# The gate row of a decoder layer: one pair of products in place of a column, a diagonal and a pair, with its result in a raw weight buffer

## The reference, cut to what matters

```
shift, scale, gate = split(silu(c) @ w_ada + b_ada, 3)
h    = rms_norm(x) * (1 + scale) + shift
proj = h @ w_in                      # q, k, v, gate_a, u, gate_b
y_a  = sliding_window_attention(q, k, v) * silu(gate_a)
y_b  = conformer_conv(u) * silu(gate_b)
y    = concat(y_a, y_b) @ w_out
out  = x + gate * y
```

## Time and profile before

| what | value |
|---|---|
| median of 3 runs | 436.16 us (434.95 to 436.86) |
| profiled execution, its own time | 439.13 us |
| its span in the profile | 437.4 us |
| mean granted TensorE clock | 0.992 |
| TensorE busy | 419.0 us (96%) |
| VectorE busy | 338.7 us (77%) |
| ScalarE busy | 206.4 us (47%) |
| GpSimd busy | 110.3 us (25%) |

### The profile page before, as it was taken

One profiled execution on the slowest core, in us unless ns is written; L12 is line 12 of the kernel. 1 busy time (PEld: TensorE's weight loads), 2 busy tenths in 40 slices (PEclk: granted clock), 3 DMA queues, 4 the chain that ended last, 5 costly groups with the idle time before them and its releaser, 6 DMA issues.

```text
span 437.4 us, 5758 instructions
## 1 busy us (share of the span) xinstructions
PE 419.0 (96%) x2059; PEld 329.5 (75%) x2059; DVE 338.7 (77%) x572; ACT 206.4 (47%) x457; POOL 110.3 (25%) x134
## 2 busy tenths in 40 slices
PE   1999997999999998999999999999999999999996
PEld 1588785888888887668766766767777888888886
DVE  3789777499999999999998797799986997322222
ACT  3445678005302038768677979624065785100000
POOL 2100050002440443354324225983022004100000
PEclk9999998999999999999999999999999999999999
DMA  7999957304950000004003285992637057951111
GB/s 245 318 299 277 334 181 237 97 0 144 224 84 1 3 10 7 9 0 151 0 2 96 55 139 112 159 115 68 125 74 120 0 191 231 262 136 48 49 48 48
DMA packets 62518, 51.39 MB, mean 117 GB/s; under 512 B 19271, under 2 KB 57467, under 8 KB 62490
## 3 DMA queue, kind: packets, MB, share of 16 engines
q1 hardware_dynamic: 46484, 41.51, 31.8%
q0 software_dynamic: 15904, 9.44, 16.2%
q10 hardware_dynamic: 102, 0.07, 0.1%
HBM read 46.82 MB, written 4.19 MB: 117 GB/s over the span
## 4 chain that ended last, share of the span: by engine, by line
PE 48%; DVE 30%; issue 4%; ACT 3%; POOL 1%; DMA 1%; DVEq 0%; ACTq 0%
PE pm L580 5%; PE pm L582 5%; PE pm L581 5%; DVE cacc L1295 4%; PE pm L840 4%; PE pm L839 4%; PE pm L838 4%; DVE cacc L1315 3%; DVE z L1315 3%; DVE z L1302 3%; PE tr L840 2%; PE tr L839 2%; PE ps L707 2%; PE tr L838 2%; PE pm L772 2%
## 5 line engine op out<-in xcount | busy, mean ns | idle before, releaser
L580 PE MATMUL pm<-h,wts 128*128 128x512 f32 x224 | 92.3, 412 | 0.8 <-DVE gb L1427 0.7
L582 PE MATMUL pm<-h,wts 128*128 128x512 f32 x224 | 88.6, 396 | 0.0
L581 PE MATMUL pm<-h,wts 128*128 128x512 f32 x224 | 88.4, 395 | 0.0
L580 PEld LDWEIGHTS pm<-h,wts 128*128 128x128 f32 x224 | 42.9, 192 | 15.8 <-issue 5.3
L582 PEld LDWEIGHTS pm<-h,wts 128*128 128x128 f32 x224 | 42.6, 190 | 9.4
L581 PEld LDWEIGHTS pm<-h,wts 128*128 128x128 f32 x224 | 42.9, 191 | 8.9 <-issue 0.7
L772 PE MATMUL pm<-wts,h 128*128 128x256 f32 (+1 forms) x128 | 45.9, 358 | 0.1
L916 ACT ACTIVATE wts<-raw 128x1024 fp32r<-128x1024 f32 x30 | 31.2, 1050 | 30.3 <-PE pm L582 17.4
L774 PE MATMUL pm<-wts,h 128*128 128x256 f32 (+1 forms) x128 | 43.1, 336 | 0.0
L773 PE MATMUL pm<-wts,h 128*128 128x256 f32 (+1 forms) x128 | 43.0, 336 | 0.0
L443 POOL DMA_DIRECT2D wts<-in_w_in x22 | 28.8, 2701 | 52.9 <-ACT wts L918 52.9
(11 more groups left out here) (204 smaller groups left out, 900.9 us busy)
## 6 DMA issues: line engine op xcount, KB each, us to landing
slab<-in_w_ada SPq DMA_DIRECT2D x16, 512.0 KB, 7.2
raw<-in_w_in SPq DMA_DIRECT2D x14, 512.0 KB, 4.7
xs<-in_x SPq DMA_DIRECT2D x8, 512.0 KB, 7.5
raw<-in_w_ada SPq DMA_DIRECT2D x8, 512.0 KB, 4.5
xr<-in_x SPq DMA_DIRECT2D x8, 512.0 KB, 5.2
out<-xr SPq DMA_DIRECT2D x15, 256.0 KB, 2.0
wts<-in_w_in POOLq DMA_DIRECT2D x6, 512.0 KB, 8.8
raw<-in_w_in SPq DMA_DIRECT2D x8, 256.0 KB, 6.1
```

The source lines that it names most:

```text
L580: pe.matmul(out, hi_w, hi_x, start=first, stop=False)
L581: pe.matmul(out, lo_w, hi_x, start=False, stop=False)
L582: return pe.matmul(out, hi_w, lo_x, start=False, stop=last)
```

## The change

The diagonal, the columns and their two instructions on VectorE are gone. GpSimd now waits for the last gate sum and starts a transfer that adds the gate's bias, from memory, to partition 0 of `gacc`. Where the eight small products stood, TensorE multiplies an all-ones matrix by `gacc`, two products of 512 columns, which give the finished row on all partitions at once. ScalarE copies it to `gbc` right away, behind `w_hi(13)`. `gbc` now lies in the third raw buffer, so that from the 23rd load on (piece 14 and later) only two raw buffers are left, used in turn: a load waits for the conversion of the piece two before it, no longer three. The pair of products among the layer norm's (`gate_row`) is gone.

```
-    gdiag = at("gdiag", [NT, P], F32, Z_AT + 8192)
-    gbc = at("gbc", [D], F32, S_AT)
+    gbc = at("gbc", [D], F32, RAW_AT + 8192)
...
+        def slot(r):
+            return r % 3 if r < 22 else (r + 1) % 2
+        def user_ahead(r):
+            return max(q for q in range(r) if slot(q) == slot(r))
...
                 if r >= 3:
-                    was, n = raws[r - 3]
+                    was, n = raws[user_ahead(r)]
...
+            gp.wait_ge(d_gp, KT)
+            gp.dma_start(gacc[0:1, :], b_ada[0:1, 2 * D:3 * D], accum_op=ALU.add).then_inc(s_bias, 16)
+
             w_lo(8)
             w_lo(9)
...
-            pe.wait_ge(d_gp, KT)
+            pe.wait_ge(s_bias, 16)
             pe.wait_ge(a_h32, 16)
-            for i in range(KT):
-                last = pe.matmul(tr[:, 0, i:i + 1], gacc[:, i * P:(i + 1) * P], ones[:, 0:1], start=True, stop=True)
-            last.then_inc(p_gcol, 1)
+            for half in range(2):
+                last = pe.matmul(tr[:, half, :], ones[:, :], gacc[:, half * HALF:(half + 1) * HALF], start=True, stop=True)
+            last.then_inc(p_gbc, 1)
...
                 if b == 0:
-                    pe.wait_ge(d_gcol, 1)
+                    pe.wait_ge(a_gbc, 1)
...
-            def gate_row():
-
-                pe.wait_ge(d_gdiag, 1)
-                pe.wait_ge(a_pt, 2 * NT)
-                for half in range(2):
-                    last = pe.matmul(tr[:, half, :], ones[:, :], gdiag[:, 4 * half:4 * half + 4, :], start=True, stop=True)
-                last.then_inc(p_gbc, 1)
...
-                        if (m, half, k) == (6, 0, 0):
-                            gate_row()
...
-            pe.wait_ge(a_gbc, 1)
             for i in range(5):
...
             for i in range(10, 14):
                 w_hi(i)
+            act.wait_ge(p_gbc, 1)
+            act.wait_ge(d_wlo, LATER.index(12) + 1)
+            act.activation(gbc[:, :].rearrange("p (a n) -> p a n", a=2), tr[:, :, :], ACT.Copy).then_inc(a_gbc, 1)
...
                     if m == 0:
-                        act.wait_ge(d_gcol, 1)
+                        act.wait_ge(p_gbc, 1)
...
-                    act.wait_ge(p_gbc, 1)
-                    act.wait_ge(p_PV, NT)
-                    act.activation(gbc[:, :].rearrange("p (a n) -> p a n", a=2), tr[:, :, :], ACT.Copy).then_inc(a_gbc, 1)
...
-            dve.wait_ge(p_gcol, 1)
-            dve.tensor_tensor(gcol[:, :], tr[:, 0, 0:KT], cols[:, C_GT:C_GT + KT], ALU.add).then_inc(d_gcol, 1)
...
-                    dve.wait_ge(p_PT, 16)
-                    dve.wait_ge(p_T, NT)
-                    dve.tensor_tensor(gdiag[:, :, :], ident[:, :].unsqueeze(1).to_broadcast([P, KT, P]),
-                                      gcol[:, :].unsqueeze(2).to_broadcast([P, KT, P]), ALU.mult).then_inc(d_gdiag, 1)
```

More of the change, by code:

```diff
@@ L133, in build @@
     bs1 = small("bs1", [KT])
-    gcol = small("gcol", [KT])
     nmx = small("nmx", [2, NH])
@@ L172, in build @@
         p_rows, p_xT, p_ada, p_main = sem("p_rows"), sem("p_xT"), sem("p_ada"), sem("p_main")
-        p_gcol, p_gbc, p_T, p_S, p_PT, p_PV = sem("p_gcol"), sem("p_gbc"), sem("p_T"), sem("p_S"), sem("p_PT"), sem("p_PV")
+        p_gbc, p_T, p_S, p_PT, p_PV = sem("p_gbc"), sem("p_T"), sem("p_S"), sem("p_PT"), sem("p_PV")
         p_mean, p_var, p_bc, p_out = sem("p_mean"), sem("p_var"), sem("p_bc"), sem("p_out")
@@ L185, in build @@
         d_cact, d_xn, d_ada, a_ab, d_hlo = sem("d_cact"), sem("d_xn"), sem("d_ada"), sem("a_ab"), sem("d_hlo")
-        d_glu, d_conv, d_gcol, d_ss, d_rope = sem("d_glu"), sem("d_conv"), sem("d_gcol"), sem("d_ss"), sem("d_rope")
+        d_glu, d_conv, s_bias, d_ss, d_rope = sem("d_glu"), sem("d_conv"), sem("s_bias"), sem("d_ss"), sem("d_rope")
         d_prod = sem("d_prod")
         d_cp, d_nmx, d_rden, d_gate, d_ya = sem("d_cp"), sem("d_nmx"), sem("d_rden"), sem("d_gate"), sem("d_ya")
-        d_gdiag, d_sq, d_dm, d_var, d_ldiag, d_e, d_v, d_yb, d_o, d_link = (
-            sem("d_gdiag"), sem("d_sq"), sem("d_dm"), sem("d_var"), sem("d_ldiag"), sem("d_e"), sem("d_v"),
+        d_sq, d_dm, d_var, d_ldiag, d_e, d_v, d_yb, d_o, d_link = (
+            sem("d_sq"), sem("d_dm"), sem("d_var"), sem("d_ldiag"), sem("d_e"), sem("d_v"),
             sem("d_yb"), sem("d_o"), sem("d_link"))
@@ L230, in build @@
         for r, (kind, i) in enumerate(raws):
-            total[r % 3] += 16 * (transfers(*pieces[i]) if kind == "w" else 1)
-            raw_due.append(total[r % 3])
+            total[slot(r)] += 16 * (transfers(*pieces[i]) if kind == "w" else 1)
+            raw_due.append(total[slot(r)])
         ADDED = [i for i, (u, p) in enumerate(pieces) if u in (4, 5, 8, 9, 10, 11, 12, 13, 14)]
@@ L273, in raw_half @@
         def raw_half(i):
-            src = raw[:, raw_at["w", i] % 3, :]
+            src = raw[:, slot(raw_at["w", i]), :]
             if i < EARLY:
@@ L342, in load_raw @@
                         sp.wait_ge(a_neg, ADDED.index(n) + 1)
-                dst = raw[:, r % 3, :]
+                dst = raw[:, slot(r), :]
                 if kind == "g":
-                    sp.dma_start(dst, w_ada[0, i * P:(i + 1) * P, 2 * D:3 * D]).then_inc(s_raw[r % 3], 16)
+                    sp.dma_start(dst, w_ada[0, i * P:(i + 1) * P, 2 * D:3 * D]).then_inc(s_raw[slot(r)], 16)
                     return
@@ L348, in load_raw @@
                 for to, src in piece_source(u, p, dst.rearrange("p (k n) -> p k n", k=4)):
-                    sp.dma_start(to, src).then_inc(s_raw[r % 3], 16)
+                    sp.dma_start(to, src).then_inc(s_raw[slot(r)], 16)
             def load_slab(k, parts=(0, 1)):
@@ L911, in w_hi @@
                 r = raw_at["w", i]
-                act.wait_ge(s_raw[r % 3], raw_due[r])
+                act.wait_ge(s_raw[slot(r)], raw_due[r])
                 if free[u]:
@@ L1248, in gate_sum @@
                 r = raw_at["g", i]
-                dve.wait_ge(s_raw[r % 3], raw_due[r])
+                dve.wait_ge(s_raw[slot(r)], raw_due[r])
                 if i == 0:
                     dve.wait_ge(p_ada, KT)
-                    ins = dve.tensor_scalar(gacc[:, :], raw[:, r % 3, :], cact[:, i:i + 1], None, ALU.mult)
+                    ins = dve.tensor_scalar(gacc[:, :], raw[:, slot(r), :], cact[:, i:i + 1], None, ALU.mult)
                 else:
                     dve.wait_ge(d_gp, i)
-                    ins = dve.scalar_tensor_tensor(out=gacc[:, :], in0=raw[:, r % 3, :], scalar=cact[:, i:i + 1],
+                    ins = dve.scalar_tensor_tensor(out=gacc[:, :], in0=raw[:, slot(r), :], scalar=cact[:, i:i + 1],
                                                    in1=gacc[:, :], op0=ALU.mult, op1=ALU.add)
```

## The result

The changed kernel takes 447.09 us (446.7 to 448.15, 4 runs) against 436.41 us before (434.95 to 436.86, 4 runs), a ratio of 1.0251 with a 95% interval of 1.0220 to 1.0283: slower by 10.7 us, where 440.2 us was forecast and 446.0 was the range's upper end.

The account below looks back on a forecast made before the run. TensorE was taken as the bound, busy 419.0 of 437.4 us. Gains of 0.5, a 3.0 us wait at the ninth output step and 1.5 of slow clock gave +4.0 on the 436.16 median: 440.2 us, range 435.4 to 446.

Parts of the forecast that it names:

- The gate's products at 130: TensorE at 130.46: two new products replace eight small ones, 1.72 us against about 1.8, gain 0.1 us.
- The pair of products at the layer norm: At 312 to 324: removing the pair saves TensorE 1.72 us, mostly lost waiting at `ln_var`; the chain gains 0.4 us.
- Bounds: 0.1 us if the clock stretch grows by the longer wait: At the layer norm: lowest gain allowed for removing diagonal and pair; upper bound 1.8 us, 0.4 taken.
- Two raw buffers in the middle: Pieces 18 to 25: each load waits for the piece two before it; counted as costing nothing.
- Two raw buffers at the end: From 364: piece 28 waits for piece 26's conversion, holding eight `xr` and piece 29; the deciding term.
- the wait of 3.0 us: TensorE at the ninth output step, from 389.6 until piece 29's addition lands at 392.6; bounds 0 to 8.6 us.
- the `xr` 11 us at the fast rate: 378: Within the landing estimate by order: the eight residual loads take 11 us behind piece 28 and end at 378.
- reckoning (b): Piece 29's landing worked out by queue order: 390.5 to 394.6, later if earlier additions are still queued.
- Reckoning (a): Piece 29's landing worked out by bytes from 364 on: 389.3 without stores, up to 396.3 with seven stores.
- Rival (3): Additions starved while `xr` run, landing near 395 to 398, waits of 6 to 8.6 us: about 444.5 us; chance 0.25.
- The clock behind the wait: Behind the ninth step's wait, 3 us at half clock cost 1.5 us, counted once; bounds 0 and 3 us.
- rival (1): Last addition lands by 389.6, so the transfer stays hidden and only 0.5 us gain is left: 435.7 us; chance 0.19.

Follow-up runs that it names:

- the three with the filler: Changed kernel, its three-buffer variant and its split-residual-load variant, each with the removed pair's products put back as ones by ones, result unused: 445.52, 434.90, 435.41 us.
- `two_buffers_only`: Kernel before, gate untouched, with only two of the three raw buffers used from the 23rd load on: 446.1 us, ratio 1.0251.
- `weights_first`: Changed kernel with piece 29's load directly behind piece 28's, ahead of all eight residual loads: 444.21 us, ratio 1.0186.
- `three_buffers_later_variance`: Changed kernel with three raw buffers throughout, gate row sent through memory, and `ln_var` two steps later in TensorE's list: 436.58 us, ratio 1.0027.

## Why the prediction was wrong

**The gate's products at 130: right.** The new pair begins at 127.84, and the second product behind it 1.94 us later, where it was 2.03 before (127.84 to 129.78, 130.46 to 132.49): the 0.1 us foreseen. From the gate's products to `ln_mean` it can't be seen: that is 183.08 us in both traces, and 182.4 to 183.3 in the other kernels. The new waits for the bias and for the copy to `gbc` cost nothing, as said: the 4 KB addition, which no row had shown, started at 79.45 and landed 4.2 us later.

**The pair of products at the layer norm: right up to `ln_var`, wrong behind it.** That the pair's 1.72 us would be lost in a wait was right (1.66 us of wait against some 1.5), and so was the small gain of VectorE's chain: `ln_var` starts 0.3 us earlier relative to `ln_mean`, where 0.4 was said. What failed is the step "Bounds: 0.1 us if the clock stretch grows by the longer wait", and the 0.4 us taken as gain. From `ln_mean` to `ln_scale` it is 20.37 us in place of 19.06, a loss of 1.3 us where at worst a gain of 0.1 had been allowed, and the difference is the length of the slow stretch. That length varies from execution to execution: the five traces in which TensorE waits some 1.66 us for the variance have 20.35 to 20.37 us (three of them) or 18.8 (two), the two with the gate's real pair 19.05 and 19.06, the three with the filler 17.2. So the step that failed is the bound; on the median, the kernels with the old pair put the worth of the filled wait at 1.6 to 2.8 us.

**Two raw buffers in the middle: right.** No wait for a late piece delays TensorE between 130 and 310, in this kernel or in `two_buffers_only`.

**Two raw buffers at the end: right in mechanism, wrong in size.** Every station was as described, each 1.3 us earlier with TensorE's list: piece 28 requested at 362.4, eight `xr`, then piece 29 at 368.6, ScalarE idle twice, TensorE waiting at the ninth step for the addition to `wts`. The term mis-sized is the wait of 3.0 us, through the landing. The step that failed is "the `xr` 11 us at the fast rate: 378". The fast rate of the earlier trace rows was read in a stretch in which q0 moved nothing; at the end the additions of pieces 26 to 28 run beside the `xr`, and these move at 0.253 MB/us: they end near 384, and piece 29 lands at 387.5, 5 to 7 us later than reckoning (b) had it, although the whole end of the list began 1.3 us sooner. The last addition then took 6.5 us, less than the 7.6 to 9.7 allowed, and landed at 396.4, where 392.6 was taken. The wait is 7.6 us in place of 3.0. TensorE got there at 388.98, 0.6 us sooner than the 389.6 reckoned. Reckoning (a) with its seven stores, set aside for (b), gave 396.3 for the landing: it counted 9.17 MB to be moved (9.42 measured). That it is right to 0.1 us is luck in part, since it has 32.3 us from piece 28's request and 34.0 were measured, but counting the bytes of both queues and the stores caught most of what the reckoning by order missed. Rival (3) had this landing and this wait, though its 444.5 us is still 2.6 short, and for the opposite reason: it had the additions standing still behind the `xr`, and they ran all the while.

**The clock behind the wait: right.** 1.5 us were counted, 1.9 measured.

**The sum.** Forecast: -0.5 + 3.0 + 1.5 = +4.0. Measured from the gate on: +1.3 + 7.7 + 1.9 = +10.9, against 10.7 between the medians. The range missed by 1.1 us, because its upper end paired the longest wait (8.6 us) with a gain of 0.5 at the top and the layer norm, where 1.3 were lost. The late `xr` cost nothing, as said: VectorE waited 6.46 us for the first, and TensorE never waited for VectorE's banks in the output steps. Some slips of the recorded working change nothing: a wait of 8.6 us belongs to a landing at 398.2 and not 398, a landing at 395 to a wait of 5.4 and not 6, and the estimate by the 3.2 us of rival (1) gives 386.1 to 388.1 and not 386.

## What to carry to other kernels

When a buffer is taken away, follow the queue that fills it: the load that now waits holds everything behind it in its list, and what is held may be bytes that had the DMA engines to themselves. Asking sooner for the urgent load gave back only 2.9 of 10.7 us; moving half of the held loads ahead of the blocked one as well, 8.9. And before counting the removal of TensorE work as a gain, ask what TensorE does in its place: if it waits, the clock can take more than the work was worth.

## What the runs showed of the hardware that was not expected

While loads and additions ran together, the two queues moved the same number of packets: from 372 to 382, 696 and 696 in the changed kernel, 701 and 702 in `weights_first`, 1050 and 1053 in the kernel before. In the changed kernel these were 2.53 MB for the `xr` and 0.68 MB for the additions. The `xr` move 4 KB rows, the weights 1 KB rows, so the queue with the larger rows got nearly four times the bytes. The Trainium skill, "DMA: Bandwidth & Descriptors", section "Queues, rings and completion order", says that an engine goes round between its queues packet by packet; these counts agree. Beside the 4 KB rows, all additions together moved at 0.068 MB/us, against 0.103 (1.03 MB in the same 10 us) in the kernel before. They share that: in `weights_first` the last one was started while that of piece 28, started 2.4 us ahead of it, was still running, and its 512 KB took 19.7 us.

The clock fell in all five traces with some 1.66 us of idleness followed by sixteen tiny products, and stayed up in the three in which the same stretch was filled. Idleness alone doesn't decide it: `three_buffers_later_variance` had a wait of 1.6 us and a clock of 1.00 from 320 to 332 in its profile, and the kernel before had only 0.20 us of it and a clock of 0.86. What else decides it was not settled.
